# 256-token products with both activation planes in one 512-column matmul, and halves added at eviction

## The chip, the cores and the metric

One core of a Trainium2 chip runs the whole program. The metric is device time of one execution in microseconds (us). TensorE multiplies; VectorE, ScalarE and GpSimd work elementwise; SyncE issues the loads of the weights.

## What is computed

Two transformer blocks one after the other, on 256 tokens of 2048 features, in f32 with f32 accuracy. The first block puts 16 meta tokens ahead (272 positions), does neighbourhood and latent attention, and ends in a gated feed-forward with a depthwise convolution. The second block has 256 positions alone. Its products are all 256 tokens wide; of the first block `up` and `down` of the feed-forward are. What surrounds the change, from the reference:

```python
def conv_glu(x, w_gate, w_up, conv_w, conv_b, w_down):          # first block
    g = x @ w_gate
    u = x @ w_up
    ...                                                         # gc: width-3 convolution of g, plus bias
    return (jax.nn.silu(gc) * u) @ w_down

        # second block
        h = rmsnorm_2(x, norm_mix_g[l]) * (1.0 + sc_m) + sh_m
        proj = h @ w_in[l]
        a_b, a_c, a_x, q, f_logit, i_in, g_out, gate_a, gate_b = jnp.split(proj, split_idx, axis=-1)
        y_a = (a_b * causal_depthwise_conv(a_c * a_x, conv_w[l])) @ w_conv_out[l]
        f = lb + (1.0 - lb) * jax.nn.sigmoid(f_logit)
        qh = jax.nn.silu(q)
        ...                                                     # o: gated linear scan of qh, 1 - f, i_in
        o = rmsnorm_2(o, gnorm_g[l]) * jax.nn.silu(g_out)
        y_b = o @ w_hgrn_out[l]
        merged = jax.nn.sigmoid(gate_a) * y_a + jax.nn.sigmoid(gate_b) * y_b
        x = x + gt_m * (merged @ w_o[l])
        h2 = rmsnorm_2(x, norm_ffn_g[l]) * (1.0 + sc_f) + sh_f
        ff = (jax.nn.silu(h2 @ w_ffn_gate[l]) * (h2 @ w_ffn_up[l])) @ w_ffn_down[l]
        x = x + gt_f * ff
```

## The kernel before

Features lie on the 128 partitions, tokens along the free dimension. A weight is the stationary operand, 128 rows by 128 columns; an activation, 256 to 272 tokens wide, streams past it. TensorE runs the fast f32r form, which keeps fewer bits than f32, so every operand is held as a high part and a low part (what the high part leaves over). A product is three matmuls into the same bank: high weight by high activation (L560), high weight by low activation (L561), low weight by high activation (L562). Each loads its weight anew.

The weights come in 447 slabs, mostly of 1 MB, in an order set by `make_plan`: SyncE loads a slab into one of three `raw` buffers, ScalarE rounds it into `wh` (L1093), VectorE subtracts to get `wl` (L1516), each in two halves; both run up to two slabs ahead of TensorE, which waits for `s_lo`. A product of 256 output features has two tiles in two banks and takes two slabs for 2048 input features, three for the 2816 of `down`, one for 1024. Products take the bank pairs 0, 1 and 2, 3 in turn, and TensorE waits before a product until the last reader of its bank has counted `s_bank`.

Every engine has one queue in order. The program of each walks the same list of products and calls `lanes.pump` at the same four ticks of a slab, where side work moves on by a step: attention in the first block, the loads and sums of the modulation (`ada`), the scan (`hgrn`). In a scan step TensorE multiplies the scaled keys and queries of one level (L808), and VectorE copies the result under a mask (L1930), and makes the operands of the level to come (L1925). The scan of head pair p runs beside the products `q`, `f`, `i`, `g` of pair p + 1, the last one beside `ac` and `ax`. After the scan's inputs come the convolution's products `ac`, `ax`, `ab`; then the gates `ga`, `gb` and the output products `ya`, `yb`; then `wo`, and the second feed-forward.

How the 256-token products leave their banks: ScalarE takes the gate of the second feed-forward through SiLU (L1366), takes `q`, `f`, `g`, `ga`, `gb` through a sigmoid (L1433, L1435, L1477) and copies `i` and `ac`; VectorE multiplies `up` (L1855), `q`, `g` (L1971), `ax`, `ab`, `ya`, `yb` straight out of the bank into what is there, and adds `down` and `wo` to the residual stream H in one operation (L1746, L1748). `down` of the second half of a feed-forward and `wo` are followed by squares on ScalarE (L1175), summed for the next norm by TensorE (L594 to L598).

## Time and profile before

| | us |
|---|---|
| median of 3 runs (2877.54 to 2886.76) | 2879.07 |
| the profiled execution | 2879.51 |
| its span, first to last instruction | 2878.2 |

| engine | busy us | share |
|---|---|---|
| TensorE, matmuls | 2775.0 | 96% |
| TensorE, weight loads (beside the matmuls) | 2707.7 | 94% |
| VectorE | 1781.9 | 62% |
| ScalarE | 1224.4 | 43% |
| GpSimd | 307.7 | 11% |

The mean granted TensorE clock was 0.978 of full. Times of rows are from the start of the span. The bar of a matmul reaches beyond the start of the next one, since matmuls are pipelined: how often they start tells the rate, the sum of their bars does not. The scan stage with its convolution lies at 1387 to 1732 us, the gate stage at 1732 to 2008, `wo` at 2008 to 2103, the second feed-forward from there to 2863.

### The profile page before, as it was taken

Reading aid. Unit: us, or ns where it says so; the run is one execution under the profiler, and the core shown is the slowest. Engines: PE = TensorE matmul, PEld = TensorE weight load, DVE = VectorE, ACT = ScalarE, POOL = GpSimd, SP = SyncE. Lnnn points to the kernel's source line nnn. Section 1 sums busy time; section 2 is a strip of 40 time slices with the busy share of each in tenths; the row PEclk is TensorE's granted clock in tenths of the full one; section 3 lists DMA queues with packets and bytes.
Section 4 is the critical chain, followed back from the end, with each engine's and each line's share of the span. In section 5 each row is a group of like instructions: output and inputs, shape, how many; then the busy total and the mean of one; then the engine's idle time right before and its main releaser. Section 6 shows DMA issues by size and latency. Waiting matters only on the chain. (4 is left out here: it accounts for less than half of the span.)

```text
span 2878.2 us, 52012 instructions
## 1 busy us (share of the span) xinstructions
PE 2775.0 (96%) x22484; PEld 2707.7 (94%) x22484; DVE 1781.9 (62%) x2461; ACT 1224.4 (43%) x1893; POOL 307.7 (11%) x517
## 2 busy tenths in 40 slices
PE   6899998989999999999999999999989999999998
PEld 6777877989999999998999999999989999999998
DVE  5534446787777677776687856677554444454454
ACT  4444454444443344443434444334444443344443
POOL 1000001321112111122100001111110000000001
PEclk9999999999999999999999999999989999999999
DMA  6322234767888888888444558888645556655563
GB/s 191 107 79 87 71 93 156 229 218 258 274 266 279 270 271 269 271 268 264 154 148 147 169 183 264 264 277 264 198 146 191 190 174 187 196 184 196 177 188 121
DMA packets 500005, 571.25 MB, mean 198 GB/s; under 512 B 26688, under 2 KB 473280, under 8 KB 499776
## 3 DMA queue, kind: packets, MB, share of 16 engines
q1 hardware_dynamic: 467968, 463.76, 49.9%
q0 software_dynamic: 31520, 103.36, 11.2%
q8 instruction: 177, 2.90, 0.4%
q10 hardware_dynamic: 288, 0.80, 0.1%
q14 instruction: 52, 0.43, 0.0%
HBM read 565.77 MB, written 2.54 MB: 197 GB/s over the span
## 5 line engine op out<-in xcount | busy, mean ns | idle before, releaser
L1516 DVE TENSOR_TENSOR wl<-raw,wh 128x1024 fp32r<-128x1024 f32 (+1 forms) x894 | 1059.8, 1204 | 728.6 <-ACT wh L1093 723.5
L560 PE MATMUL ps<-xx,wh 128*128 128x256 f32 (+2 forms) x5104 | 1465.5, 287 | 45.4 <-DVE xx L1571 20.3
L561 PE MATMUL ps<-xx,wh 128*128 128x256 f32 (+2 forms) x5104 | 1445.7, 283 | 0.0
L562 PE MATMUL ps<-xx,wl 128*128 128x256 f32 (+2 forms) x5104 | 1442.3, 283 | 0.0
L1093 ACT ACTIVATE wh<-raw 128x1024 fp32r<-128x1024 f32 (+1 forms) x894 | 880.3, 1029 | 651.4 <-PE ps L562 647.5
L560 PEld LDWEIGHTS ps<-xx,wh 128*128 128x128 f32 x5104 | 972.1, 190 | 60.1 <-issue 36.0
L561 PEld LDWEIGHTS ps<-xx,wh 128*128 128x128 f32 x5104 | 972.8, 191 | 1.4 <-issue 1.0
L562 PEld LDWEIGHTS ps<-xx,wl 128*128 128x128 f32 x5104 | 972.4, 191 | 0.0
L561 PE MATMUL ps<-hid,wh 128*128 128x256 f32 x1408 | 394.9, 280 | 0.0
L560 PE MATMUL ps<-hid,wh 128*128 128x256 f32 x1408 | 394.0, 280 | 0.0
L562 PE MATMUL ps<-hid,wl 128*128 128x256 f32 x1408 | 393.4, 279 | 0.0
L964 POOL DMA_DIRECT2D ada_raw<-in_w_ada x384 | 206.7, 538 | 1220.7 <-DVE ada_acc L1718 1105.4
L1718 DVE SCALAR_TENSOR_TENSOR ada_acc<-ada_raw,small,ada_acc 128x512 f32<-128x512 f32 x360 | 268.6, 746 | 0.3 <-DMA ada_raw<-in_w_ada 0.2
L560 PEld LDWEIGHTS ps<-hid,wh 128*128 128x128 f32 x1408 | 265.3, 188 | 0.0
L561 PEld LDWEIGHTS ps<-hid,wh 128*128 128x128 f32 x1408 | 264.4, 188 | 0.0
L562 PEld LDWEIGHTS ps<-hid,wl 128*128 128x128 f32 x1408 | 263.6, 187 | 0.0
L1376 ACT ACTIVATE hid<-gc 128x256 fp32r<-128x256 f32 x88 | 36.8, 418 | 215.9 <-DVE gc L1855 215.9
L909 POOL TENSOR_TENSOR ssq_h<-ssq_h,sqt 128x256 f32<-128x256 f32 (+1 forms) x28 | 20.6, 737 | 726.4 <-ACT sqt L1175 724.6
L1855 DVE TENSOR_TENSOR gc<-ps,gc 128x256 f32<-128x256 f32 x88 | 37.1, 421 | 69.8 <-PE ps L562 69.8
L1857 DVE TENSOR_TENSOR hid<-gc,hid 128x256 fp32r<-128x256 f32 x88 | 37.5, 426 | 42.6 <-ACT hid L1376 42.6
L1363 ACT ACTIVATE gc<-ps,vec 128x256 f32<-128x256 f32 x44 | 22.4, 561 | 77.4 <-PE ps L562 77.4
L1366 ACT ACTIVATE gc<-ps 128x256 f32<-128x256 f32 x44 | 14.5, 380 | 76.4 <-PE ps L562 76.4
(298 smaller groups left out, 2055.9 us busy)
## 6 DMA issues: line engine op xcount, KB each, us to landing
raw<-in_w_in SPq DMA_DIRECT2D x118, 1024.0 KB, 5.3
ada_raw<-in_w_ada POOLq DMA_DIRECT2D x384, 256.0 KB, 4.8
raw<-in_w_gate SPq DMA_DIRECT2D x44, 1024.0 KB, 6.0
raw<-in_w_up SPq DMA_DIRECT2D x44, 1024.0 KB, 6.6
raw<-in_w_ffn_gate SPq DMA_DIRECT2D x44, 1024.0 KB, 5.1
raw<-in_w_ffn_up SPq DMA_DIRECT2D x44, 1024.0 KB, 5.1
raw<-in_w_down SPq DMA_DIRECT2D x32, 1024.0 KB, 6.0
raw<-in_w_ffn_down SPq DMA_DIRECT2D x32, 1024.0 KB, 5.6
```

The lines of the kernel that those rows point to most:

```text
L560: pe.matmul(dst, h[:, c, o:o + w], x[:, 0, k, g.t0:g.t1], start=(k == 0), stop=False)
L561: pe.matmul(dst, h[:, c, o:o + w], x[:, 1, k, g.t0:g.t1], start=False, stop=False)
L562: m = pe.matmul(dst, l[:, c, o:o + w], x[:, 0, k, g.t0:g.t1], start=False, stop=end)
L909: pool.tensor_tensor(acc, acc, bufs[(i - 1) % len(bufs)][:, 0:m], ALU.add).then_inc(s_sp[who], 1)
L964: pool.dma_start(ada_raw[i % NADA][:, :], w[:, k, 512 * g:512 * g + 512]).then_inc(s_ada[i % NADA], 16)
L1093: act.activation(wh[i % NS][:, part], raw[i % NR][:, part], ACT.Copy).then_inc(s_hi, 1)
L1363: act.activation(gc[:, :], src[:, 2:258], ACT.Identity, bias=V("cb", n), scale=V("cw1", n)).then_inc(s_gca, 1)
L1376: act.activation(hid[:, 0, 2 * g + j, :], gct[u % NGC][:, :], ACT.Copy).then_inc(s_hidh, 1)
L1516: dve.tensor_tensor(wl[i % NS][:, part], raw[i % NR][:, part], wh[i % NS][:, part].bitcast(F32), ALU.subtract).then_inc(s_lo, 1)
L1718: dve.scalar_tensor_tensor(out=ada_acc[:, :], in0=r, scalar=s, in1=ada_acc[:, :], op0=ALU.mult, op1=ALU.add).then_inc(s_acc, 1)
L1855: dve.tensor_tensor(gc[:, :], ps[2 + j][:, 0:256], gc[:, :], ALU.mult).then_inc(s, 1)
L1857: dve.tensor_tensor(hid[:, 1, 2 * g + j, :], gc[:, :], hid[:, 0, 2 * g + j, :].bitcast(F32), ALU.subtract).then_inc(s_hidl, 1)
```

## The change

For products 256 tokens wide the high weight is multiplied once: its moving operand is the 256 columns of the high activation followed by the 256 of the low one, 512 columns, into both halves of a bank. The low weight by the high activation still goes into the first half. The order of the two matmuls is turned round in the last triple, so that a full-width matmul both begins and ends the accumulation. Narrow products of 258 and 272 columns stay as they are.

A bank now holds two halves that are to be added. VectorE does that: `join` reduces the bank over its two halves into an SBUF tile, and ScalarE's SiLU, sigmoids and copies of such products read the tile, or are gone (`i`, `ac`). New semaphores order these (`s_qg`, `s_fs`, `s_sg`, `s_um` and others); two tiles `joined` lie over buffers that are idle at the time. Where VectorE multiplied out of a bank it now joins first and multiplies then. A residual (`residual_halves`) becomes two `scalar_tensor_tensor` in a row, the second waiting for the first. In the second feed-forward SiLU on ScalarE moves from straight behind the gate's product to the first tick of `up`, as it was in the first one.

The convolution's part, ScalarE's part of the feed-forwards and the declarations are left out here; they follow the same pattern.

```diff
+        joined = [ssq["b"][:, 0:SEQ], sqt[0][:, 0:SEQ]]
...
                         for j, (o, w) in enumerate(g.tiles):
+                            if n == SEQ:
+                                both = ps[g.banks[j]][:, :].rearrange("p (a b) -> p a b", a=2)
+                                x2 = x[:, :, k, g.t0:g.t1]
+                                if not end:
+                                    pe.matmul(both, h[:, c, o:o + w], x2, start=(k == 0), stop=False)
+                                m = pe.matmul(ps[g.banks[j]][:, 0:n], l[:, c, o:o + w], x[:, 0, k, g.t0:g.t1], start=False, stop=False)
+                                if end:
+                                    m = pe.matmul(both, h[:, c, o:o + w], x2, start=False, stop=True)
+                                if c == nk - 1 and j == len(g.tiles) - 1:
+                                    m.then_inc(s_slab, 1)
+                                continue
                             dst = ps[g.banks[j]][0:w, 0:n]
...
                     if lv == 0:
-                        for j in range(2):
-                            pe.wait_ge(*last_use(("q", p), j))
+                        pe.wait_ge(s_qg, 4 * p + 2)
...
-                    act.wait_ge(s_slab, done(key))
-                    if p >= 2 and n == "q":
-                        act.wait_ge(s_ohl, 2 * (p - 2) + 2)
                     for j in range(2):
-                        src, dst = ps[GEMMS[key].banks[j]][:, 0:SEQ], set_of(p)[n][:, j, :]
-                        s, _ = last_use(key, j)
-                        if n == "i":
-                            act.activation(dst, src, ACT.Copy).then_inc(s, 1)
-                        elif n == "f":
-                            act.activation(dst, src, ACT.Sigmoid).then_inc(s, 1)
-                        else:
-                            act.activation(dst, src, ACT.Sigmoid).then_inc(s_sig, 1)
+                        x = set_of(p)[n][:, j, :]
+                        if n == "f":
+                            act.wait_ge(*last_use(key, j))
+                            act.activation(x, x, ACT.Sigmoid).then_inc(s_fs, 1)
+                        elif n != "i":
+                            act.wait_ge(*last_use(key, j))
+                            if p or n == "g":
+                                act.wait_ge(s_qg, 4 * p + 2 * "qg".index(n) - 1 + j)
+                            act.activation(joined[j], x, ACT.Sigmoid).then_inc(s_sig, 1)
...
-                    if g >= 2:
-                        act.wait_ge(s_mg, 2 * (g - 2) + 2)
                     for n, buf in zip(("ga", "gb"), sgbuf[g % 2]):
-                        key = (n, g)
-                        gemm(key)
-                        act.wait_ge(s_slab, done(key))
-                        if g == 0:
-                            act.wait_ge(s_ocl, 8)
+                        gemm((n, g))
                         for j in range(2):
-                            s, _ = last_use(key, j)
-                            act.activation(buf[:, j, :], ps[GEMMS[key].banks[j]][:, 0:SEQ], ACT.Sigmoid).then_inc(s, 1)
+                            act.wait_ge(*last_use((n, g), j))
+                            act.activation(buf[:, j, :], buf[:, j, :], ACT.Sigmoid).then_inc(s_sg, 1)
...
+            def join(key, j, dst):
+                s, _ = last_use(key, j)
+                both = ps[GEMMS[key].banks[j]][:, :].rearrange("p (a b) -> p b a", a=2)
+                dve.wait_ge(s_slab, done(key))
+                dve.tensor_reduce(dst, both, AX.X, ALU.add).then_inc(s, 1)
+
+            firsts = [0]
+
+            def residual_halves(key, j, c, scale=1.0):
                 s, use = last_use(key, j)
-                new = ps[GEMMS[key].banks[j]][:, 0:T - t0]
+                dst = H[:, c, 16:T]
+                dve.scalar_tensor_tensor(out=dst, in0=ps[GEMMS[key].banks[j]][:, SEQ:2 * SEQ], scalar=scale, in1=dst, op0=ALU.mult, op1=ALU.add).then_inc(s_first, 1)
+                firsts[0] += 1
+                dve.wait_ge(s_first, firsts[0])
+                dve.scalar_tensor_tensor(out=dst, in0=ps[GEMMS[key].banks[j]][:, 0:SEQ], scalar=scale, in1=dst, op0=ALU.mult, op1=ALU.add).then_inc(s, 1)
...
+                        else:
+                            for j in range(2):
+                                u = first_use + j
+                                dve.wait_ge(s_hidl, u - NGC + 1)
+                                join(gate, j, gct[u % NGC][:, :])
                         gemm(up)
-                        dve.wait_ge(s_slab, done(up))
+                        for j in range(2):
+                            join(up, j, joined[j])
                         for j in range(2):
                             u = first_use + j
                             gc = gct[u % NGC]
-                            s, _ = last_use(up, j)
-                            if b == 1:
-                                dve.wait_ge(s_silu, u + 1)
-                            else:
-                                dve.wait_ge(*last_use(gate, j))
-                            dve.tensor_tensor(gc[:, :], ps[2 + j][:, 0:256], gc[:, :], ALU.mult).then_inc(s, 1)
+                            dve.wait_ge(s_silu, u + 1)
+                            dve.wait_ge(*last_use(up, j))
+                            dve.tensor_tensor(gc[:, :], joined[j], gc[:, :], ALU.mult).then_inc(s_um, 1)
+                        for j in range(2):
+                            u = first_use + j
+                            gc = gct[u % NGC]
                             dve.wait_ge(s_hidh, u + 1)
                             dve.tensor_tensor(hid[:, 1, 2 * g + j, :], gc[:, :], hid[:, 0, 2 * g + j, :].bitcast(F32), ALU.subtract).then_inc(s_hidl, 1)
                     for g in range(8):
                             c = 2 * g + j
                             if f == 1:
                                 dve.wait_ge(*last_use((b, "down", 0, g), j))
-                            residual((b, "down", f, g), j, c, 16, mod[:, 80 + c:81 + c] if b == 2 else None)
+                            residual_halves((b, "down", f, g), j, c, mod[:, 80 + c:81 + c] if b == 2 else 1.0)
...
+                    if p >= 2 and n == "q":
+                        dve.wait_ge(s_ohl, 2 * (p - 2) + 2)
                     for j in range(2):
-                        d, src, c = set_of(p)[n][:, j, :], ps[GEMMS[key].banks[j]][:, 0:SEQ], 2 * p + j
-                        s, use = last_use(key, j)
+                        join(key, j, set_of(p)[n][:, j, :])
+                    for j in range(2):
+                        d, c = set_of(p)[n][:, j, :], 2 * p + j
                         if n == "f":
-                            dve.wait_ge(s, use)
+                            dve.wait_ge(s_fs, c + 1)
                             dve.tensor_scalar(d, d, oml[:, c:c + 1], lb[:, c:c + 1], ALU.mult, ALU.add).then_inc(s_hf, 1)
                         elif n != "i":
                             sig += 1
                             dve.wait_ge(s_sig, sig)
-                            dve.tensor_tensor(d, src, d, ALU.mult).then_inc(s, 1)
+                            dve.tensor_tensor(d, joined[j], d, ALU.mult).then_inc(s_qg, 1)
...
+                    for j in range(2):
+                        join(("ya", g), j, merged[:, 2 * g + j, :])
                     for j in range(2):
                         c = 2 * g + j
-                        s, _ = last_use(("ya", g), j)
-                        dve.wait_ge(*last_use(("ga", g), j))
-                        dve.tensor_tensor(merged[:, c, :], ps[GEMMS[("ya", g)].banks[j]][:, 0:SEQ], ga[:, j, :], ALU.mult).then_inc(s, 1)
+                        dve.wait_ge(*last_use(("ya", g), j))
+                        dve.wait_ge(s_sg, 4 * g + j + 1)
+                        dve.tensor_tensor(merged[:, c, :], merged[:, c, :], ga[:, j, :], ALU.mult).then_inc(s_ma, 1)
                     gemm(("yb", g))
-                    dve.wait_ge(s_slab, done(("yb", g)))
+                    if g:
+                        dve.wait_ge(s_gm, 2 * g)
+                    for j in range(2):
+                        join(("yb", g), j, joined[j])
                     for j in range(2):
                         c = 2 * g + j
-                        s, use = last_use(("yb", g), j)
-                        dve.wait_ge(*last_use(("gb", g), j))
-                        dve.tensor_tensor(gb[:, j, :], ps[GEMMS[("yb", g)].banks[j]][:, 0:SEQ], gb[:, j, :], ALU.mult).then_inc(s, 1)
-                        dve.wait_ge(s, use)
+                        dve.wait_ge(*last_use(("yb", g), j))
+                        dve.wait_ge(s_sg, 4 * g + 2 + j + 1)
+                        dve.tensor_tensor(gb[:, j, :], joined[j], gb[:, j, :], ALU.mult).then_inc(s_gm, 1)
+                    for j in range(2):
+                        c = 2 * g + j
+                        dve.wait_ge(s_ma, c + 1)
+                        dve.wait_ge(s_gm, c + 1)
                         dve.tensor_tensor(merged[:, c, :], merged[:, c, :], gb[:, j, :], ALU.add).then_inc(s_mg, 1)
...
-                    residual(("wo", g), j, c, 16, mod[:, 32 + c:33 + c])
+                    residual_halves(("wo", g), j, c, mod[:, 32 + c:33 + c])
```

## Rows read from the trace of the kernel before

**Rows 1.** The page, totals: busy us, share of the span and instructions of each engine
```profile
PE 2775.0 (96%) x22484; PEld 2707.7 (94%) x22484; DVE 1781.9 (62%) x2461; ACT 1224.4 (43%) x1893; POOL 307.7 (11%) x517
```

**Rows 2.** Stretches: length; busy us (instructions) PE, PEld, DVE, ACT, POOL; clock; DMA share, GB/s
```profile
2232.60:2243.85 11.25, 11.25 (x98) 11.25 (x97) 6.33 (x8) 4.75 (x6) 0.00 (x0) 1.00 0.56 187
1489.90:1504.80 14.90, 14.90 (x131) 14.90 (x130) 14.35 (x28) 4.55 (x6) 0.00 (x0) 1.00 0.43 142
2007.80:2019.10 11.30, 11.30 (x99) 11.30 (x98) 10.92 (x22) 4.75 (x6) 3.76 (x7) 1.00 0.79 250
2030.30:2046.60 16.30, 13.97 (x107) 13.76 (x106) 9.45 (x12) 4.71 (x6) 1.48 (x2) 0.90 0.67 200
```

**Rows 3.** Groups by form: line engine op, out<-in, shape xcount | busy us, mean ns
```profile
L560 PE MATMUL ps<-xx,wh 128*128 128x256 f32 x3776 | 1071.8, 284 | 18.8 <-DVE xx L1569 16.8 <-POOL xx L895 2.0
L560 PE MATMUL ps<-hid,wh 128*128 128x256 f32 x1408 | 394.0, 280 | 0.0
L560 PE MATMUL ps<-conv,wh 128*128 128x256 f32 x128 | 35.9, 280 | 0.0
```

**Rows 4.** Timeline of TensorE: start us, us, engine line op; 90 intervals in each pair
```profile
2233.10 0.28 PE L560 MATMUL ps<-xx,wh 128*128 128x256 f32 x1
...
2243.62 0.28 PE L560 MATMUL ps<-xx,wh 128*128 128x256 f32 x1
...
2446.03 0.28 PE L561 MATMUL ps<-hid,wh 128*128 128x256 f32 x1
...
2456.63 0.28 PE L561 MATMUL ps<-hid,wh 128*128 128x256 f32 x1
...
45.30 0.30 PE L561 MATMUL ps<-xx,wh 128*128 128x272 f32 x1
...
56.56 0.29 PE L561 MATMUL ps<-xx,wh 128*128 128x272 f32 x1
```

**Rows 5.** Timeline of TensorE in a stretch granted 1.2 GHz
```profile
1384.15 0.42 PE L561 MATMUL ps<-xx,wh 128*128 128x256 f32 x1
1384.36 0.41 PE L562 MATMUL ps<-xx,wl 128*128 128x256 f32 x1
```

**Rows 6.** Weight loads by form; then matmuls on 64-column weights, 42 intervals apart
```profile
L560 PEld LDWEIGHTS ps<-cqx,wh 128*64 128x64 f32 x32 | 4.4, 136 | 0.0
L560 PEld LDWEIGHTS ps<-hid,wh 128*128 128x128 f32 x1408 | 265.3, 188 | 0.0
...
69.30 0.29 PE L561 MATMUL ps<-xx,wh 128*64 128x272 f32 x1
...
74.55 0.29 PE L561 MATMUL ps<-xx,wh 128*64 128x272 f32 x1
```

**Rows 7.** The scan's plain f32 matmul, two records each: timeline, then group by form
```profile
1467.24 1.02 PE L828 MATMUL ps<-hK,cst 128*128 128x512 f32 x2
...
L828 PE MATMUL ps<-hK,cst 128*128 128x512 f32 x8 | 4.1, 593 | 0.0
```

**Rows 8.** VectorE's groups by form: reduction out of a bank, operations of two widths
```profile
L1644 DVE TENSOR_REDUCE lc<-ps 128x1 f32<-128x272 f32 x16 | 7.0, 440 | 15.3 <-ACT out_b L1230 13.5 <-PE ps L662 1.9
L1718 DVE SCALAR_TENSOR_TENSOR ada_acc<-ada_raw,small,ada_acc 128x512 f32<-128x512 f32 x360 | 268.6, 746 | 0.3 <-DMA ada_raw<-in_w_ada 0.2
L1748 DVE SCALAR_TENSOR_TENSOR H<-ps,mod,H 128x256 f32<-128x256 f32 x48 | 21.0, 480 | 38.7 <-PE ps L562 38.7
```

**Rows 9.** Timeline of the scan stage behind product q: VectorE, then TensorE's level step
```profile
1492.50 0.74 DVE L1971 TENSOR_TENSOR hg_q<-ps,hg_q 128x256 f32<-128x256 f32 x2
...
1495.61 0.42 DVE L1925 TENSOR_TENSOR hK<-hg_k,hR 128x256 f32<-128x256 f32 x1
...
1497.47 0.38 PE L808 MATMUL ps<-hQ,hK 128*128 128x128 f32 x2
```

**Rows 10.** Timeline of ScalarE in product wo 2, idle time before an instruction in brackets
```profile
2034.42 0.42 ACT L1175 ACTIVATE sqt<-H 128x256 f32<-128x256 f32 x1 [4.24 <-DVE H L1748]
...
2035.13 1.99 ACT L1093 ACTIVATE wh<-raw 128x1024 fp32r<-128x1024 f32 x2
```

83 lines of the change are left out of this document (44 added, 39 removed).

## The prediction

> **What bounds the kernel now.** I read the views in this order. First the totals of the page [rows 1]: TensorE is busy 96% of the span, VectorE 62%, ScalarE 43%. A matmul's bar outlasts its turn, so a busy share is no proof, and I went to the starts. The stage table [rows 2] shows one product of the second feed-forward, an `up`, in 11.25 us, with the engine covered throughout at full clock (PEclk 1.00) and VectorE busy 6.33 us of it. The starts themselves [rows 4] are evenly spaced: 90 intervals of the 256-column form take 10.52 us, or 116.9 ns each, and 96 of them make 11.22 us. So nothing but the rate at which matmuls follow each other sets that stage, and slabs, ScalarE and VectorE are ahead. The same even pace stands in both feed-forwards and most of the gate stage. Two places are different, and they decide what the change costs: the scan stage, where VectorE is busy 14.35 of 14.90 us while TensorE is just as full, and the start of `wo`, 10.92 of 11.30 us, followed by a product that takes 16.30 us instead of 11.2 [rows 2].
>
> **The matmuls.** The form groups [rows 3] count the affected triples by the first matmul of each: 3776 on `xx`, 1408 on `hid`, 128 on `conv`, and as many on `oo`, which feeds as many products, 5440 in all (the 258- and 272-column products are left as they are). Each triple is now three matmuls of 256 columns with three weight loads. It becomes one of 512 and one of 256, with two loads: as many columns, one instruction fewer. The question is what the instruction costs beside its columns. At the 2.4 GHz level 256 columns are 106.7 ns. The interval is 116.9 ns on `xx` (10.2 over) and 10.60 us / 90 = 117.8 ns on `hid` (11.1 over); with 272 columns (113.3 ns) it is 11.26 / 90 = 125.1 ns, 11.8 over [rows 4]. At the 1.2 GHz level the two neighbouring starts are 0.21 us apart, which is 256 / 1.2 with nothing over [rows 5]. Is the surplus that of the weight load? A load of 64 columns takes 136 ns against 188 for 128, yet the 272-column matmuls on half-width weights start 5.25 / 42 = 125.0 ns apart, as those on full width do [rows 6]. So a shorter load gives nothing back, and a load with more time to hide in need not either. Is it per column or per matmul? Widths of 256 and 272 are too near each other to say: 11 ns each, or 9% of the columns, fit both. The only 512-wide matmul of the trace is plain f32, which streams its columns twice: the pair takes 1.02 us and the second one 0.593, so they start 0.43 us apart, 1024 / 2.4 = 427 ns plus 3 [rows 7]. There the cost did not grow with width. That is the nearest row for a wide matmul, and I take the surplus as fixed: a triple becomes 213.3 + 106.7 + 2 surpluses. Gain: 3776 x 10.2 + 1664 x 11.1 ns = 38.5 + 18.5 = **57 us**. Bounds: nothing, if the surplus goes with the columns or if the two-part operand (256 columns of the high plane, then 256 of the low one) starts twice; and 57 + 5440 x 7.7 = 99 us if a 512-column matmul carries only the 3 ns of the f32 one.
>
> **The joins.** Every evicted tile of the gate, `up`, scan, tap and gate products is now summed by a reduction over 2 x 256 elements. The nearest rows [rows 8]: a reduction of 272 elements out of a bank takes 440 ns; an operation of 512 elements takes 746 where one of 256 takes 480, so 1.04 ns an element. 440 + 240 x 1.04 = **690 ns** a join. The elements are read 256 apart, which no row shows; the upper bound is two steps an element, 1.2 us. ScalarE loses its reads of the banks and works on what is joined; it is idle more than half of the time, and I count that at nothing except where VectorE waits for it. In a feed-forward a gate-`up` pair takes four joins at most, 2.8 us, on a VectorE that is busy 6.33 of 11.25 us [rows 2]; a join comes after slabs have been split two ahead, and a bank is next written one product (11 us) later. So they are hidden in the second feed-forward, and in the first too, where only `up` is joined. The cover would be gone at about 11 us of lateness.
>
> **Scan stage.** Four times (for p = 1, 2, 3 and during `ac`, `ax`) the level steps run beside two products with VectorE full. TensorE takes its step at 1497.47, and VectorE's operand for it stands at 1495.61 + 0.42 = 1496.03: 1.4 us of slack [rows 9]. Behind the `q` product the multiplication at 1492.50 is now preceded by two joins (some 1.3 us), and it waits for a sigmoid that starts only when a join ended and that may stand behind a split on ScalarE (two of them take 1.99 us [rows 10]); queued behind that wait are the slab's low half and the next level, for which TensorE waits. That is 1.6 to 2.8 us against 1.4 us of slack; behind `f` come two joins more. I take 1.7 us of stall each time, **7 us** in all; bounds 0 and 14 (both joins and waits in full, twice per p).
>
> **Start of `wo`.** VectorE gets eight more joins in `ya` and `yb` of the last two groups, is full in `wo` 0 already, and the 5 us hole in `wo` 2 comes as ScalarE's next two splits (2035.13) stand behind a square that waited 4.24 us for VectorE's residual [rows 10]. Its lateness grows by some joins and by two additions: **5 us**, bounds 1 and 9.
>
> **Ends of stages.** A residual is two dependent `scalar_tensor_tensor` of 480 ns instead of one operation. Inside a stage that is hidden; at the ends of `down` (twice) and `wo` the last pair stands ahead of the norm: two extra, overlapped at 0.4 us, and waits, 1 us each, **3 us**; bounds 2 and 4.
>
> **Sum.** The profiled execution took 2879.5 us (span 2878.2), half a microsecond above the median 2879.07. 2879.5 - 57 + 7 + 5 + 3 = **2837.5 us**. The case's own range is 2823 to 2852, from the bounds of the three losses and half a nanosecond of the surplus.
>
> **The rivals.**
> *Columns carry the surplus* (or the two-part operand starts twice): the triple stays at 351 ns and the additions remain. 2879.5 + 15 = 2894.5 us, up to 2907 with the losses at their bounds. It decides from 228 ns for the 512-column matmul: then a triple saves 6 ns and nearly half of the gain is gone; from about 231 ns the saving, under 3 ns a triple, no longer covers the 15 us of losses and the kernel is slower. For it: the surplus grew from 10.2 to 11.8 with 16 more columns. Against it: the f32 pair, and that the surplus vanishes at the lower clock. Chance 0.22.
> *A long stream sheds the surplus*: everything that streams for 213 ns or more in these rows has 0 to 3 ns over (256 columns at 1.2 GHz, the f32 pair). If so, a triple is 216 + 117 and the time 2837.5 - 42 = 2796 us. Against it: half the load time changed nothing at 272 columns. Chance 0.15. The Trainium skill, "TensorE: Matmul & The Clock Gate", section "Wait — 56ns, not 53.3ns?", gives N / 2.4 GHz plus a fixed 2.5 ns between starts; by it the 512-column matmul comes to 216 ns and this rival would hold. For 256 columns the trace shows 116.9 where that rule has 109.2, so I don't trust it for this kind of matmul.
> *Slow joins*: the strided read makes a join 1.2 us, 0.5 more. In the scan stage the stalls grow by about 4 us each (eight joins per p), 16 us, and by 6 us at `wo`: 2860 us. Nothing in the trace speaks for it, and nothing excludes it. Chance 0.13. The Trainium skill, "SBUF — State Buffer", says that a bank's lines are 8 bytes and that non-contiguous access to it costs throughput; it says so of matmuls, and no row here shows it for VectorE.
> *The forecast*: chance 0.50.
>
> **How the numbers follow.** A difference under 0.3% (8.6 us, 2870.4 to 2887.7) can't be told from no change here. Faster by more: the forecast, the long stream, and slow joins for the most part: 0.74. Within: slow joins at their worst, or a half-gained surplus, 0.06. Slower: the column rival but for its mildest form, 0.20. The range has to hold 8 in 10. The forecast's own range holds half of the chance, so it reaches down to the long stream and up to the column rival with its losses at the middle: 2793 to 2899.
>
> **What the profile after would show.** In the second feed-forward, an `up` product in 11.25 - 32 x 0.0102 = 10.92 us and starts 224 ns after a 512-column matmul, 117 after a 256-column one; 10880 matmuls in place of 16320. A join at 690 ns. In the scan stage TensorE with idle time put down to VectorE, 1 to 2 us per p; a longer hole in `wo`. The prediction is wrong if the interval after a 512-column matmul is over 228 or under 220 ns, if joins take over 0.9 us, or if VectorE's lateness in the first feed-forward, where it also adds up the modulation, reaches the slab splits and shows as TensorE's wait on L1516.

## The result and the profile after

The changed kernel takes 2896.76 us (median; 2888.68 to 2900.33), the kernel before 2880.64 us on the same chip: 1.0053 times as long, 95% interval 1.0046 to 1.0060. It is slower by 16 us where I had forecast 42 us less; 2896.76 us is the time of the column rival (2894.5 to 2907). The profiled execution took 2888.68 us (span 2887.3), 9 us more than that of before.

The totals of the page after (as [rows 1]) and the stretches that answer to [rows 2], in the same order: an `up` product, `f` of the scan stage, `wo` 0, `wo` 2.

```profile
PE 2772.2 (96%) x17044; PEld 2458.7 (85%) x17044; DVE 1955.3 (68%) x2793; ACT 1223.1 (42%) x1877; POOL 307.4 (11%) x517
```

```profile
2254.20:2265.40 11.20, 11.20 (x66) 9.80 (x66) 5.92 (x6) 4.63 (x6) 0.00 (x0) 1.00 0.59 185
1486.10:1502.90 16.80, 15.02 (x99) 13.36 (x98) 15.57 (x29) 4.74 (x6) 0.00 (x0) 1.00 0.39 125
2011.75:2024.70 12.95, 12.42 (x66) 9.74 (x65) 12.76 (x26) 4.54 (x6) 3.77 (x7) 1.00 0.73 228
2036.00:2055.00 19.00, 14.94 (x75) 12.96 (x73) 12.06 (x16) 6.43 (x8) 1.47 (x2) 0.82 0.57 171
```

5440 instructions are gone from TensorE (22484 - 17044) and its busy time has hardly moved. The first line is the whole disappointment: an `up` product of 64 matmuls takes 11.20 us where one of 96 took 11.23. The other three show the losses: TensorE, full in `f` and in `wo` 0 before, now stands idle 1.8 us of 16.8 and 0.5 of 12.95, and `wo` 2 has grown from 16.3 to 19.0 us.

TensorE's starts in that `up` product, as in [rows 4] (start us, bar us):

```profile
2254.38 0.39 PE L568 MATMUL ps<-xx,wh 128*128 128x512 f32 x1
2254.61 0.28 PE L569 MATMUL ps<-xx,wl 128*128 128x256 f32 x1
...
2264.53 0.39 PE L568 MATMUL ps<-xx,wh 128*128 128x512 f32 x1
```

From the first to the last wide matmul shown are 29 pairs: 10.15 / 29 = 350 ns for a pair, against 3 x 116.9 = 351 for three narrow ones. The wide one holds the engine 0.23 us; over its 5002 intervals in the trace at full clock and without gaps the mean is 231.4 ns. The forecast had 224, and over 228 was one of its signs of being wrong.

The joins and second residual halves (as [rows 8]), and what TensorE waits for in the scan stage, where before it waited for no level step (us in total, how many waits, the longest in us):

```profile
L1740 DVE TENSOR_REDUCE ssq_b<-ps 128x256 f32<-128x512 f32 x60 | 41.5, 691 | 82.4 <-PE ps L571 82.3
L1750 DVE SCALAR_TENSOR_TENSOR H<-ps,mod,H 128x256 f32<-128x256 f32 x48 | 23.2, 484 | 1.7
```

```profile
PE ps L823 <- DVE hK L1939: 4.3, 4, 1.8
PE ps L831 <- DVE hK L1950: 3.3, 4, 2.6
```

I summed the time from one product's end (the count that its last matmul makes) to the next one's, stage by stage (us; early is all before the first feed-forward, "end" what comes behind the last product; the columns behind the first are differences from before; "again" is a second profile of the changed kernel, e10):

| stage | before | changed | again (e10) | narrow, with joins (e2) | wide alone (e3) | weights moved (e7) | packed (e8) | packed, wide (e9) | packed, same place (e12) |
|---|---|---|---|---|---|---|---|---|---|
| early | 583.0 | -2.8 | +7.2 | -0.4 | +1.9 | +2.2 | +1.4 | +5.0 | +0.2 |
| first feed-forward | 775.9 | -2.6 | -2.6 | 0.0 | -2.6 | -3.7 | -3.6 | -0.9 | -3.6 |
| scan, conv | 373.7 | +10.1 | +12.8 | +10.1 | -1.6 | -0.7 | -7.2 | +0.6 | +6.6 |
| gates | 275.5 | -0.7 | -0.7 | 0.0 | -0.7 | -2.6 | -3.6 | +0.7 | +1.9 |
| `wo` | 94.9 | +4.6 | +4.4 | +4.0 | +1.2 | +0.1 | -0.7 | +2.7 | +0.2 |
| second feed-forward | 760.4 | -0.5 | -0.4 | +1.6 | -2.3 | -9.5 | -23.8 | +2.2 | +3.8 |
| end | 14.8 | +1.0 | +1.0 | +1.0 | 0.0 | 0.0 | 0.0 | 0.0 | 0.0 |

The early stage has no 256-token product, and the change leaves its matmuls as they were; where its time differs most, so does the granted clock (e10 below).

### The profile page after: what moved, and what is told of

Same layout as the page of the kernel before. It is cut to its first block and busy times, and to the rows that moved or that the text cites. A ratio compares the mean times of both kernels' runs of the same rounds, so it can differ in the third digit from the quotient of the medians.

```text
span 2887.3 us, 41573 instructions
## 1 busy us (share of the span) xinstructions
PE 2772.2 (96%) x17044; PEld 2458.7 (85%) x17044; DVE 1955.3 (68%) x2793; ACT 1223.1 (42%) x1877; POOL 307.4 (11%) x517
## 5 line engine op out<-in xcount | busy, mean ns | idle before, releaser
L568 PE MATMUL ps<-xx,wh 128*128 128x512 f32 x3540 | 1265.4, 398 | 21.8 <-DVE xx L1565 17.0
L569 PE MATMUL ps<-xx,wl 128*128 128x256 f32 x3776 | 1047.2, 282 | 0.0
L568 PEld LDWEIGHTS ps<-xx,wh 128*128 128x128 f32 x3540 | 669.2, 189 | 176.0 <-issue 14.8
L569 PEld LDWEIGHTS ps<-xx,wl 128*128 128x128 f32 x3776 | 714.0, 189 | 9.5 <-issue 1.0
L568 PE MATMUL ps<-hid,wh 128*128 128x512 f32 x1344 | 472.5, 394 | 0.0
L576 PE MATMUL ps<-xx,wh 128*128 128x258 f32 (+2 forms) x1328 | 392.6, 296 | 25.3 <-DVE xx L1567 19.0
L577 PE MATMUL ps<-xx,wh 128*128 128x258 f32 (+2 forms) x1328 | 386.0, 291 | 0.0
L578 PE MATMUL ps<-xx,wl 128*128 128x258 f32 (+2 forms) x1328 | 385.0, 290 | 0.0
L979 POOL DMA_DIRECT2D ada_raw<-in_w_ada x384 | 206.7, 538 | 1225.4 <-DVE ada_acc L1714 1113.2
L568 PEld LDWEIGHTS ps<-hid,wh 128*128 128x128 f32 x1344 | 252.8, 188 | 57.4
L576 PEld LDWEIGHTS ps<-xx,wh 128*128 128x128 f32 (+1 forms) x1328 | 256.3, 193 | 36.6 <-issue 19.9
L577 PEld LDWEIGHTS ps<-xx,wh 128*128 128x128 f32 (+1 forms) x1328 | 256.9, 193 | 1.3
L578 PEld LDWEIGHTS ps<-xx,wl 128*128 128x128 f32 (+1 forms) x1328 | 256.8, 193 | 0.0
L571 PE MATMUL ps<-xx,wh 128*128 128x512 f32 x236 | 88.1, 395 | 0.0
```

Of the source, the lines that this page charges most:

```text
L568: pe.matmul(both, h[:, c, o:o + w], x2, start=(k == 0), stop=False)
L569: m = pe.matmul(ps[g.banks[j]][:, 0:n], l[:, c, o:o + w], x[:, 0, k, g.t0:g.t1], start=False, stop=False)
L571: m = pe.matmul(both, h[:, c, o:o + w], x2, start=False, stop=True)
L576: pe.matmul(dst, h[:, c, o:o + w], x[:, 0, k, g.t0:g.t1], start=(k == 0), stop=False)
L577: pe.matmul(dst, h[:, c, o:o + w], x[:, 1, k, g.t0:g.t1], start=False, stop=False)
L578: m = pe.matmul(dst, l[:, c, o:o + w], x[:, 0, k, g.t0:g.t1], start=False, stop=end)
```

## Experiments

**Rates alone (e1).** What does a matmul cost by width, type, pieces and place? A kernel that runs nothing but stretches of 96 matmuls of one shape, each stretch this loop with its own width and start:

```python
for i in range(96):
    o = start + 1088 * (i // 6 % 2)          # in elements
    mm = pe.matmul(ps[0][:, 0:256], wall[:, 128 * (i % 32):128 * (i % 32) + 128], xall[:, o:o + 256], start=(i == 0), stop=(i == 95))
```

> Not this kernel's computation at all: 28 stretches of 96 matmuls each on TensorE, one shape per stretch, nothing else running, so that each stretch reads one spacing. In f32r with 128-column weights it takes widths 128, 192, 256, 320, 384, 448 and 512 in one piece, 512 in two pieces (69.6 KB... that is 17408 bytes apart, as the high and low activations lie, and 1088 bytes apart), 512 in four pieces, 256 in two pieces, 256 and 512 with one and the same weights and with four banks in turn, 256 with the operand's start 16, 32, 64, 128 and 192 bytes past a 256-byte boundary, 512 at 64, 128 and 192, and then bf16 and plain f32 at 256 and 512. Theory A (each column of an f32r operand costs a little more than 1/2.4 ns: the surplus grows with the columns): 256 columns 117 ns apart, 512 about 234 ns apart, in one piece or two; 128 columns about 59. Theory B (each piece of an operand pays a start of about 10 ns): 512 in one piece 223 ns apart, in two pieces 233, in four 253; 256 in two pieces 127. Theory C (the surplus is fixed for each matmul, and something else in the kernel lengthened the wide ones): 512 at 223 ns in one piece and in two. Theory D (the surplus belongs to one weight load for each matmul): 256 columns with the same weights at 107 to 110 ns.

TensorE's timeline, one row for each stretch (start us, length us). A row's spacing is the next row's start less its own, divided by 96. First by width, all from a 256-byte boundary, in one piece (L156 to L180); then 512 columns in two pieces 17408 bytes apart (L184), in two 1088 apart (L188), in four (L192):

```profile
60.65 10.84 PE L156 MATMUL ps<-xall,wall 128*128 128x128 f32 x96
71.33 10.91 PE L160 MATMUL ps<-xall,wall 128*128 128x192 f32 x96
82.07 11.70 PE L164 MATMUL ps<-xall,wall 128*128 128x256 f32 x96
93.61 14.24 PE L168 MATMUL ps<-xall,wall 128*128 128x320 f32 x96
107.69 16.80 PE L172 MATMUL ps<-xall,wall 128*128 128x384 f32 x96
124.33 20.00 PE L176 MATMUL ps<-xall,wall 128*128 128x448 f32 x96
144.17 21.97 PE L180 MATMUL ps<-xall,wall 128*128 128x512 f32 x96
165.97 21.92 PE L184 MATMUL ps<-xall,wall 128*128 128x512 f32 x96
187.73 22.55 PE L188 MATMUL ps<-xall,wall 128*128 128x512 f32 x96
210.12 21.96 PE L192 MATMUL ps<-xall,wall 128*128 128x512 f32 x96
231.91 11.68 PE L196 MATMUL ps<-xall,wall 128*128 128x256 f32 x96
...
321.43 11.36 PE L220 MATMUL ps<-xall,wall 128*128 128x256 f32 x96
332.63 11.04 PE L224 MATMUL ps<-xall,wall 128*128 128x256 f32 x96
343.51 11.55 PE L228 MATMUL ps<-xall,wall 128*128 128x256 f32 x96
354.90 11.08 PE L232 MATMUL ps<-xall,wall 128*128 128x256 f32 x96
365.81 22.15 PE L236 MATMUL ps<-xall,wall 128*128 128x512 f32 x96
```

128 and 192 columns are 111 and 112 ns apart, 256 are 120.2, 320 are 146.7, 384 are 173.3, 448 are 206.7, 512 are 227.1. The last part of the figure has 256 columns that start 32, 64, 128 and 192 bytes past the boundary (L220 to L232): 116.7, 113.3, 118.6, 113.6. So the same 256 columns cost 6.7 to 13.5 ns beside their 106.7, by where they start. For 512 columns the surplus is 13.8 ns from the boundary and 20.0 from byte 192. Two and four pieces give 226.7 and 227.0, as one does, but two at different places of a line 233.2: theory B, a start for each piece, is out. The same weights for every matmul change nothing (120.0), nor do four banks in turn. That is not yet an answer to theory D: those stretches too have 96 weight loads for their 96 matmuls, so what a load itself costs is not shown. No theory fits all: from the boundary the surplus is the same at 256, 320, 384 and 512 columns, 13.3 to 13.8 ns (C), but 20.0 at 448; from byte 192 it grows from 7 to 20 (A). In bf16 the spacing was 109.2 and 215.9 ns, and in plain f32 2 x 107.9 and 2 x 214.6 for one matmul: surpluses of 1.2 to 2.6 that do not grow with width (each at one start only). The Trainium skill, "TensorE: Matmul & The Clock Gate", section "Back-to-back issue gap", has N / 2.4 + 2.5 ns for the gap of matmuls by themselves; the bf16 stretches agree with that to 0.1 ns, and the f32r ones do not, by 4 to 18 ns.

**Evictions alone (e2).** The changed kernel with the wide matmul taken apart:

```diff
-if not end:
-    pe.matmul(both, h[:, c, o:o + w], x2, start=(k == 0), stop=False)
-m = pe.matmul(ps[g.banks[j]][:, 0:n], l[:, c, o:o + w], x[:, 0, k, g.t0:g.t1], start=False, stop=False)
-if end:
-    m = pe.matmul(both, h[:, c, o:o + w], x2, start=False, stop=True)
+pe.matmul(bank[:, 0:n], h[:, c, o:o + w], x[:, 0, k, g.t0:g.t1], start=(k == 0), stop=False)
+pe.matmul(bank[:, n:2 * n], h[:, c, o:o + w], x[:, 1, k, g.t0:g.t1], start=False, stop=False)
+m = pe.matmul(bank[:, 0:n], l[:, c, o:o + w], x[:, 0, k, g.t0:g.t1], start=False, stop=end)
```

> The changed kernel's evictions with the matmuls taken apart again: high weights by high activations into the first half of the bank, high weights by low activations into the second half, low weights by high activations into the first, each 256 columns wide. The joins, the new waits and the split residuals stay. If the wide matmul gains nothing (spacing 234 ns for it and 117 for a narrow one), this kernel takes as long as the changed one: 2895 to 2899 us, and all of the 16 us over the kernel before belongs to VectorE's part. If the wide matmul itself is what costs (a slower triple than before), this one is nearer to 2881 us. If the wide one does gain and the evictions cost more than the 15 us that I had added, this one is well above: 2905 us or more.

2895.74 us, 1.0055 (1.0035 to 1.0075) times the kernel before: as long as the changed one. The losses are those of VectorE's part. Product `f` with p = 2 in it:

```profile
1491.30:1508.10 16.80, 15.17 (x131) 14.97 (x130) 15.57 (x30) 4.74 (x6) 0.00 (x0) 1.00 0.38 126
```

The same 16.80 us with 131 matmuls as with 99: the rate of TensorE has no part in what that product takes.

**Wide matmuls alone (e3).** The other half: the changed kernel's matmul block, put into the kernel before, whose evictions stay.

```diff
+if n == SEQ:
+    ...                      # the block of the change, unaltered
+    continue
 dst = ps[g.banks[j]][0:w, 0:n]
```

> The kernel before with the wide matmuls alone: the 512-column matmul of high and low activations into both halves of a bank, but evictions, waits and residuals as they were, which read only the first half (so the product of high weights and low activations is left out of the result in the 256-token products). If the wide matmul gains nothing: 2876 to 2884 us, within 0.2% of the kernel before. If it gains what I had predicted for it (57 us less): 2824 us. If it costs by itself: above 2886 us.

2875.25 us, 0.9979 (0.9969 to 0.9989): a gain, but of 5 us and not 57. By kind of product it is small sums of both signs: the `down` products (`hid`) 1.0 us less for eight in the first feed-forward and 1.3 in the second, `up` of the first 0.3 less for eleven, and of the second feed-forward's products on `xx` the second eleven `gate` 0.4 and the first eleven `up` 0.5 more, the second eleven `up` 0.2 less. 5 us less and 15 us more leave 10; the changed kernel's own median is 16 above, and e10 shows where more can come from.

**One piece (e4).** Does the two-part operand cost?

```diff
-hid = sb("hid", [P, 2, HALF, SEQ], F32R)
+hid = sb("hid", [P, HALF, 2, SEQ], F32R).rearrange("p c a t -> p a c t")
```

> The changed kernel with the hidden activations of the feed-forward laid out so that the high and low halves of a slab lie side by side: the wide operand is then one piece of 512 columns in the down products (1408 wide matmuls), and two pieces elsewhere as before. If a second piece costs a start of about 10 ns: a down product of 88 triples drops by 0.9 us, from 15.36 to about 14.5 us, and the whole by 14 us, to about 2882 us. If the surplus goes by columns: the down products stay at 15.36 us and the whole within 2 us of the changed kernel, 2893 to 2899 us.

2893.39 us (1.0041, 1.0028 to 1.0055). The `down` products take 126.09 and 123.11 us for eight, to 0.02 us what they take in the changed kernel with two pieces. With e1 the rival's second reason is out, for pieces that lie at the same place of a 256-byte line, as they do in this kernel.

**Addresses (e5).** The kernel's own pattern of 12 slabs, two tiles and three matmuls, with nothing beside it, on chosen starts and strides.

```python
def narrow(n, x0, step, gap, w0):
    for k in range(12):
        o = (x0 + step * k) // 4
        for j in range(2):
            w = w0 // 4 + 256 * (k % 6) + 128 * j
            yield from [(w, o, n), (w, o + gap // 4, n), (w + 2048, o, n)]
```

> Not this kernel's computation: stretches of 48 or 72 f32r matmuls on TensorE and nothing beside them. First 256 columns from one and the same place, the start moved in steps of 16 bytes through a 256-byte line, then 512 columns in steps of 32 bytes; then the kernel's own pattern of two tiles by three matmuls over 12 slabs, with the strides and starts of its operands (slabs 1088 bytes apart from 192; 1024 bytes apart from 192), then with other starts and with slabs 1152 and 1280 bytes apart; the same for 272 and 258 columns; and the pair of a 512- and a 256-column matmul on such operands. Theory A (the surplus over one column in 1/2.4 ns depends on where in a 256-byte line the operand starts, and not on the width): 256 columns at 113.3 ns for starts of 64 and 192, 120 for 0, 116.7 for 32; the pattern with every slab at 64 or 192 three times 113.3 = 340 ns for a triple, that with 1088 bytes between slabs 350; a wide pair 347 at 0 and 347 at 192. Theory B (the surplus depends on the step from one operand to the next, and what the stretches before showed of the start was chance): the pattern at 192 with equal steps stays at the 353 ns for a triple that the kernel has in its down products.

The pattern with slabs 1088 bytes apart from 192 took 351.5 ns for a triple, and that of the hidden activations (1024 apart from 192, weights at 128) 353.3 (L229): both within 1 ns of the whole kernel [rows 4]. So the spacing of the three narrow matmuls needs nothing else of the kernel. Then one thing changes: the same operand with the weights at 0 of a 256-byte line (L231).

```profile
336.88 8.59 PE L227 MATMUL ps<-xall,wall 128*128 128x256 f32 x72
345.32 8.64 PE L229 MATMUL ps<-xall,wall 128*128 128x256 f32 x72
353.79 8.32 PE L231 MATMUL ps<-xall,wall 128*128 128x256 f32 x72
361.95 8.32 PE L233 MATMUL ps<-xall,wall 128*128 128x256 f32 x72
```

From L229 to L231 are 8.47 us, from there to L233 8.16: 353 and 340 ns for each of 24 triples. A 512- and a 256-column matmul took 346.7 to 353.3. For this pair the stretches miss the whole kernel by more: at the place of the hidden activations 353.3 ns, where a `down` product of the changed kernel has 349.3 (15.37 us for 44 pairs). Theory A, the operand's start alone, is not enough, and theory B, the step alone, is wrong: the place of the weights counts. Nor is the place in the line all: with the operand at 192 and the weights at 128, as in L229, the low part 13312 bytes behind the high one instead of 22528 gave 340 ns (L279), though both distances are multiples of 256.

```profile
561.06 8.33 PE L279 MATMUL ps<-xall,wall 128*128 128x256 f32 x72
569.22 8.64 PE L281 MATMUL ps<-xall,wall 128*128 128x256 f32 x72
```

**The grid (e6).** Operand and weights through the line in steps of 32 bytes, 64 pairs for each stride.

> Not this kernel's computation: stretches of 72 f32r matmuls of 256 columns in the kernel's pattern of two tiles by three matmuls over 12 slabs, nothing beside them. The operand's start and the weights' start each go through a 256-byte line in steps of 32 bytes, once with slabs 1024 bytes apart and the low part 22528 bytes behind (as the hidden activations lie) and once with 1088 and 17408 (as the normed ones do); then some pairs again in another order. Theory A (where operand and weights lie together sets the spacing): each pair of starts gives the same spacing each time, 353.3 ns for three matmuls at 192 with weights at 128 and 340.0 ns with weights at 0, in whatever order they come. Theory B (the spacing depends on what ran before, not on the addresses alone): the pairs that come again give other values than the first time. With 1088 bytes between slabs all starts of the operand are gone through anyway, so 350 to 352 ns wherever it begins.

With slabs 1024 bytes apart a triple took, by (operand start less weights' start) modulo 256: 360.0 ns at 0, in all eight pairs; 356.0 at 128; 352 to 360 elsewhere; and at 192, 64 bytes short of the weights, 340.0 in four pairs of eight and 353.3 in the others. With 1088 bytes between slabs, 350 to 355 everywhere. At that one place theory B has its part, in both directions: with the operand at 64 and the weights at 128 the grid gave 340.0 and the same pair later 353.3 three times; with the operand at 192 and the weights at 0 the grid gave 353.3, and the same pair later, between others, 340.0 each time:

```profile
1204.40 8.64 PE L447 MATMUL ps<-xall,wall 128*128 128x256 f32 x72
1212.88 8.32 PE L449 MATMUL ps<-xall,wall 128*128 128x256 f32 x72
1221.04 8.64 PE L451 MATMUL ps<-xall,wall 128*128 128x256 f32 x72
1229.52 8.80 PE L453 MATMUL ps<-xall,wall 128*128 128x256 f32 x72
1238.15 8.34 PE L455 MATMUL ps<-xall,wall 128*128 128x256 f32 x72
1246.33 8.32 PE L457 MATMUL ps<-xall,wall 128*128 128x256 f32 x72
```

(L449, L455 and L457 are that pair, L451 has the operand at 64, L453 at 0.)

**In the whole kernel: the weights moved (e7).** The kernel before with one line moved up; it shifts the weights and `xx` by 384 bytes and leaves `hid`, `conv` and `oo` where they were.

```diff
+mod = sb("mod", [P, 96])
 raw = [sb(f"raw{i}", [P, SLAB]) for i in range(NR)]
 ...
-mod = sb("mod", [P, 96])
```

> The kernel before with one small tensor (384 bytes) allocated first instead of later, so that the weights start at a multiple of 256 bytes and the normed activations 64 bytes past one instead of 192; the hidden activations stay at 192. Nothing else differs. If the addresses of operand and weights together set the spacing, the 1408 triples on the hidden activations go from 353.3 to 340.0 ns, 19 us less, and perhaps those on the convolution's and the scan's outputs, which start at 192 as well (2 us more): 2859 to 2863 us. If the spacing does not follow them in the whole kernel: 2878 to 2883 us.

2863.22 us, 0.9936 (0.9919 to 0.9952). The second feed-forward's `down` products fell from 15.55 to 14.96 us, 340.0 ns for each of 44 triples:

```profile
2437.30:2452.30 15.00, 15.00 (x135) 15.00 (x134) 7.42 (x8) 5.60 (x6) 0.00 (x0) 1.00 0.61 193
```

The first one's gave 1.8 us for eight instead of 4.7: products 4 and 5 took 14.96, products 1, 2 and 7 stayed at 15.55, with no wait of TensorE in either. The place has two paces here too.

**Packed (e8).** Can the products on `xx` have it? In the second block only tokens 16 to 271 are used, so its activations can lie 1024 bytes apart in the same memory.

```diff
+xs = xx[:, :, :, :].rearrange("p a k t -> p (a k t)")[:, 48:8240].rearrange("p (a k t) -> p a k t", a=2, k=KD)
+OPERAND = {X0: xx, XS: xs, ...}
-add((n, p), "w_in_2", 0, 16, c0 + 256 * p, 256, X0, 16, T)
+add((n, p), "w_in_2", 0, 16, c0 + 256 * p, 256, XS, 0, SEQ)
```

> The kernel before with the 384-byte tensor first, as in the run before this one, and with the normed and merged activations of the second block written 1024 bytes apart (in the same memory, from byte 192 on) instead of 1088: 3072 more triples then lie as the hidden activations do, 64 bytes short of the weights' place in a 256-byte line. If the place of operand and weights sets the spacing: their triples go from 351.0 to 340.0 ns, 34 us less than with the weights moved alone, 2827 to 2835 us; each gate, up, q, f and wo product that TensorE bounds takes 10.88 us instead of 11.23. If the transfer of the weights or VectorE takes over as the bound: 2840 to 2863 us.

2841.58 us, 0.9858 (0.9842 to 0.9874): 39 us less than before, by addresses alone. An `up` product takes 10.88 us, a `down` 14.96. It is 22 us under the run before it where I expected 34. In the second feed-forward the gain is nearly whole (14.3 us beside 44 x 0.35 = 15.4); the scan stage gives 6.5 of its 9.9 (28 products of 32 triples at 11 ns). Most of what is missing there is that `q`, `f` and `i` with p = 2 and the first `ac`, `ax` and `ab` gain nothing or 0.1 us: `f` takes 14.88 us with p = 2 and 14.51 with p = 1 and 3. TensorE waits for nothing in either; its matmuls start 117.7 ns apart in the first and 113.5 in the others, the same two paces. The gate stage gives 1.0 of 5.6, since seven of its 16 `ga` and `gb` products take 11.31 us (353 ns a triple) instead of 10.88 and most of `ya` and `yb` fell back to 5.65 us from 5.45, the other pace of that place; and in `wo` seven products gain 0.35 us each and `wo` 2 takes 17.96 us instead of 16.36: TensorE's wait there (on `wo` in the next section) is 3.4 us in this kernel, 2.3 in the kernel before.

**Wide matmuls at the good place (e9).** The same addresses under the matmuls of e3.

> The same addresses with the wide matmuls, and the evictions as in the kernel before, which read only the first half of a bank (the product of high weights and low activations is left out in the 256-token products). If a 512- and a 256-column matmul do not profit from this place (356.2 ns for the pair in the stretches alone, 350.7 ns in the whole kernel): 10.7 to 16.2 ns more on each of 4608 triples, 49 to 75 us more than three narrow matmuls at the same place, 2878 to 2904 us. If the wide form were worth its fixed surplus at every place: 2 us to 60 us less than three narrow ones.

2885.74 us, 1.0012 (1.0003 to 1.0022) times the kernel before and 44 us above the packed kernel. `up` 11.29 us and `down` 15.53: 353 ns for a pair at a place where three narrow ones take 340. The wide form has no share in the gain. (The 356.2 ns of the expectation stand in no stretch: the pair's highest there was 353.3.)

**A place for the wide form (e11).**

> Not this kernel's computation: stretches of 24 pairs of a 512-column and a 256-column f32r matmul, the operand's start going through a 256-byte line in steps of 32 bytes, with the weights at 0 and at 128; the high and the low part 22528 bytes apart, then side by side, then with slabs 1088 bytes apart; last the three narrow matmuls with the parts 16384 bytes apart. If the pair has a good place as three narrow matmuls have one: 340 to 346 ns at some start, and the change would only have needed other addresses. If it has none: 349 to 358 ns everywhere, within 2% of the kernel's own 351 ns whatever the place, and 3% or more above the 340 ns of three narrow ones. For the narrow ones: 340.0 ns again where the operand starts 64 bytes short of the weights' place, 360 ns where it starts at the same place.

Over 48 combinations of starts and gaps a pair took 346.7 to 353.9 ns. The best, 346.7, came at operand starts of 32 and 160, and of 0 with the parts side by side and the weights at 0, and with 1088 bytes between slabs at no start (349 to 353). Of the two narrow stretches at the good place one took 340.0 ns and the other 353.4; both at the weights' own place took 360.0. None of the pairs reaches 340, yet neither of the two outcomes that I had written down holds: the best is 2% above 340, not 3. An estimate from these numbers: 4.0 ns less on each of 5440 pairs (350.7 to 346.7) is 22 us, more than the 15 us that the joins cost, so at that place the changed kernel might have come out some us ahead of the kernel before, and still behind three narrow matmuls at their own good place, which need no joins. No kernel with its operands there was run.

**The control (e12).** The packed block 192 bytes earlier, at the weights' own place:

```diff
-xs = xx[...].rearrange("p a k t -> p (a k t)")[:, 48:8240]...
+xs = xx[...].rearrange("p a k t -> p (a k t)")[:, 0:8192]...
```

> The kernel with packed activations as before, but the packed block begins 192 bytes earlier, so that its slabs start at the same place of a 256-byte line as the weights. Nothing else differs from the packed kernel. If the place sets the spacing: the 3072 triples go from 340.0 to 360.0 ns, 11.52 us for a gate or up product of the second feed-forward instead of 10.88; where TensorE bounds (the 44 gate and up products, the 16 gate and 8 output products: 2176 triples) that is 43 us, and with part of it in the scan stage 2880 to 2903 us, slower than the kernel before although its slabs are packed. If the packing itself made the gain: 2839 to 2845 us again.

2889.49 us, 1.0038 (1.0024 to 1.0052). A stretch of `up` products at the good place and one at the bad place (a whole product takes 10.88 and 11.52 us):

```profile
2226.80:2238.00 11.20, 11.20 (x101) 11.20 (x100) 4.72 (x4) 4.56 (x6) 0.00 (x0) 1.00 0.58 191
...
2252.60:2264.10 11.50, 11.50 (x98) 11.50 (x97) 4.72 (x4) 4.57 (x6) 0.00 (x0) 1.00 0.57 187
```

101 matmuls touch 11.20 us in the packed kernel, 98 touch 11.50 us here. 192 bytes of offset are worth 48 us, three times what the whole change moved the time.

**The changed kernel again (e10).**

> The changed kernel as it is, beside the others on one chip: 2892 to 2899 us. Its first profile spans 2887.3 us, below every other execution of it. If the first products (spans before the second block) hold the difference, with the clock lower there, then a profile of 2895 us shows the same product times from 700 us on; if it lies with VectorE's joins, the scan stage and the output projection differ.

2896.38 us (1.0046, 1.0031 to 1.0061); this profile spans 2899.9 us. Of the 12.6 us over the first profile, 10.0 lie ahead of the first feed-forward, 6.7 of them in the twelve attention products, with a granted clock of 0.92 against 0.94 over those 600 us. In the scan stage 2.7 more, and they too come with the clock: `q` 0 takes 1.2 us more, at a clock of 0.73 over that product against 0.82 (0.70 before), and `ab` 0 takes 1.5 more. In both profiles TensorE waits 2.58 us in `ab` 0 for VectorE (L831); only in this one does the clock fall behind the wait. The 20 us around it, first profile, then this one:

```profile
1626.00:1646.00 20.00, 17.42 (x103) 14.90 (x102) 15.71 (x20) 8.85 (x13) 0.00 (x0) 1.00 0.31 105
1640.00:1660.00 20.00, 18.39 (x99) 15.86 (x100) 13.82 (x17) 8.45 (x13) 0.00 (x0) 0.91 0.32 105
```

The profile of e4 shows the same 12.7 us in the scan stage as this one. The feed-forwards, gates and `wo` agree to 0.2 us. So the first profile was a short one, and so is e2's in the scan stage: 15.5 us by its median, 16.4 by its profile, is the added cost where the clock stays up behind `ab` 0's wait. Why the early stage more often has a lower clock in the changed kernel, whose matmuls there are the same, was not found, so the 5 us or so between 10 and 16 are only in part accounted for.

## Why the prediction was wrong

*The matmuls.* The step that failed is "I take the surplus as fixed": a surplus of 10 ns for the 512-column matmul, where it measured 18 (231.4 - 213.3). The 57 us rested on a plain-f32 pair [rows 7], and in f32r the surplus depends on place: over the four starts that `xx` goes through it averages 10 ns at 256 columns and 17 at 512 (e1). A pair pays 18 + 12 where a triple paid 3 x 10. Measured gain: 5 us (e3). I had the row that spoke against it, 16 more columns and 1.6 ns more, and gave it to the rival. The rival was right by luck: the surplus does not go by columns either (13.5 ns at 256, 13.8 at 512 from a boundary). What came out is its number, 2894.5 us with 15 us of losses, and its point of decision, 231 ns.

*Pieces and weight loads.* A second piece at the same place of a line costs nothing (e1, e4). Whether the weights differ from one matmul to the next does not matter either (e1); what the load itself costs was not tested. But the place of the weights counts, which I had not asked.

*The scan stage.* Predicted 7 us, measured 10.1 (e2): `f` 4.4, `ab` 2.7, `q` and `i` 1.1 each, `ac` and `ax` 0.8. The mechanism is as described: in `f` with p = 2 the level step waits for the operand behind the joins,

```profile
1495.63 1.16 PE L823 MATMUL ps<-hQ,hK 128*128 128x128 f32 x8 [1.78 <-DVE hK L1939]
```

1.78 us, and 1.71 with p = 3, where I had 1.7; with p = 1 and during `ax` it is 0.5 and 0.2. The step that I had not listed is the scan's last one, in `ab` 0:

```profile
1630.48 0.71 PE L831 MATMUL ps<-hQ,hK 128*128 128x128 f32 x4 [2.58 <-DVE hK L1950]
```

With it that product went from 13.57 to 16.26 us. I had also put the clock at nothing: in e4 and e10 it falls behind this wait and costs 1.5 us more.

*`wo`.* Predicted 5, measured 4.0 (e2): 1.4 in `wo` 0 and 2.6 in `wo` 2. The size came out, my reading of the hole did not. The splits of [rows 10] start at 2035.13, behind it. TensorE's one wait in `wo` 2 stands in front of the eight small matmuls that take up the sum of the modulation, before and after:

```profile
2032.91 1.05 PE L632 MATMUL ps<-cst,ada_acc 128*128 128x1 f32 x8 [2.33 <-DVE ada_acc L1718]
...
2040.43 1.87 PE L648 MATMUL ps<-cst,ada_acc 128*128 128x1 f32 x8 [4.06 <-DVE ada_acc L1714]
```

VectorE adds to that sum between the slabs' low halves, these wait for ScalarE's splits, and the splits stood behind a square that waited for the residual of `wo` 0, before and after:

```profile
2024.06 0.42 ACT L1171 ACTIVATE ssq_h<-H 128x256 f32<-128x256 f32 x1 [8.21 <-DVE H L1748]
...
2031.06 0.42 ACT L1186 ACTIVATE ssq_h<-H 128x256 f32<-128x256 f32 x1 [10.50 <-DVE H L1750]
```

So the lateness of VectorE is the cause, as I had said, but it works through the residual of `wo` 0. Of the 2.6 us the wait is 1.7; the small matmuls, which in the changed kernel run at the low clock (0.82 over `wo` 2 against 0.90), take 0.8 more.

*Ends.* Predicted 3, measured 2.8 (e2): the norm ahead of the second feed-forward 1.6, that ahead of `q` 0 0.2 (counted in the scan stage; 1.4 in e10, at nearly the clock of before), and 1.0 behind the last product. *Joins.* 690 ns predicted, 681 to 691 measured by tile; that reading the halves 1 KB apart costs nothing is not shown by itself, as no join of neighbouring elements was run. *Hidden parts.* In both feed-forwards and the gate stage the joins cost 0.0 us apart from that norm (e2), as costed. The losses sum to 16.7 us (10.1, 4.0, 1.6, 1.0) against 15; the forecast fell with one term.

## What to carry to other kernels

A matmul's spacing at 256 columns and f32r has an address in it: before merging or splitting matmuls, measure the exact pair in a stretch by itself, at the kernel's own strides and starts. Three narrow matmuls had there the spacing of the whole kernel within a nanosecond; the wide pair was off by up to 4 ns, and a pace of the good place did not always carry over. A price taken from another element type is none. And where TensorE is full, the start of operand and weights within a 256-byte line is worth trying first: one line of allocation gave 17 us, a packed view 22 more, and the 512-column form with its joins -16.

## What the hardware showed

At full clock most settled spacings in f32r from a 256-byte boundary are multiples of 6.67 ns: 120.0, 146.7, 173.3, 206.7, 226.7 (18, 22, 26, 31 and 34 of them), and so are 113.3 and 233.3 at other starts (17 and 35). Others are not: at the place of the hidden activations each interval is 117 to 119 ns and three make 353.3, and other starts gave 118.6 and 234.3. The bf16 stretches, at one start each, had 2.5 ns over their columns at both widths. 128 and 192 columns took 111 and 112 ns. Two relative places, the operand 64 bytes short of the weights and 64 bytes past them, have two paces, 340 and 353 ns a triple; what chooses between them wasn't found, and it costs the packed kernel part of its gain (`f`, `ga`, `gb`, `ya`, `yb`, the first `down`). Why place counts at all, whether through reads of weights and operand that meet, was not tested.
